# Columns of the modulation on TensorE: three more folded pairs, ten of VectorE's rows in the fold's bank, and a new order of VectorE's steps

## The reference, cut to what matters

```
cond = silu(c)
mod = cond @ w_ada[l] + b_ada[l]          # 2048 -> 6 * 2048
sh1, sc1, g1, sh2, sc2, g2 = split(mod)
u = x * (1 + sc1) + sh1
y = mixer(u)                              # layer 0: pooling and gated linear attention
x = layer_norm(ALPHA * x + (1 + g1) * y)
u = x * (1 + sc2) + sh2
y = conv_ffn(u)
x = layer_norm(ALPHA * x + (1 + g2) * y)
```

## Time and profile before

| | us |
|---|---|
| median of 3 runs | 2245.31 (2243.19 to 2245.43) |
| the profiled execution | 2243.39 |
| its span, first to last instruction | 2241.6 |
| TensorE busy in the span | 2208.9 |
| VectorE busy | 1683.4 |
| ScalarE busy | 1017.8 |

### The profile page before, as it was taken

One profiled execution on the slowest core, in us unless ns is written; L12 is line 12 of the kernel. 1 busy time (PEld: TensorE's weight loads), 2 busy tenths in 40 slices (PEclk: granted clock), 3 DMA queues, 4 the chain that ended last, 5 costly groups with the idle time before them and its releaser, 6 DMA issues.

```text
span 2241.6 us, 27926 instructions
## 1 busy us (share of the span) xinstructions
PE 2208.9 (99%) x11177; PEld 1836.6 (82%) x11177; DVE 1683.4 (75%) x1671; ACT 1017.8 (45%) x1050; POOL 15.6 (1%) x23
## 2 busy tenths in 40 slices
PE   7999999999999999999999999999999999999999
PEld 3778777788888888888788888878888888888886
DVE  2899999778878878788887767685788755565565
ACT  2445344454533444443455544445545334454432
POOL 1000000000000000000000000000000000000000
PEclk9999999999999999999999999999999999999999
DMA  9999899968889888789887877866688766556652
GB/s 377 385 406 350 308 329 353 318 212 276 298 300 355 301 276 288 261 281 331 309 292 277 293 260 248 309 217 190 210 275 300 258 203 197 189 187 190 236 186 102
DMA packets 392907, 612.70 MB, mean 273 GB/s; under 512 B 21229, under 2 KB 205221, under 8 KB 391750
## 3 DMA queue, kind: packets, MB, share of 16 engines
q1 hardware_dynamic: 387994, 608.34, 77.7%
q10 hardware_dynamic: 4336, 2.33, 0.3%
q0 software_dynamic: 448, 0.25, 0.0%
HBM read 608.71 MB, written 2.13 MB: 273 GB/s over the span
## 4 chain that ended last, share of the span: by engine, by line
PE 58%; DVE 1%; issue 0%; ACT 0%; DVEq 0%; ACTq 0%
PE banks L1654 32%; PE banks L1805 14%; PE banks L1813 7%; PE banks L1690 1%; PE banks L2130 1%; DVE w_lo L1050 0%; PE banks L2225 0%; PE banks L2192 0%; PE banks L2213 0%; PE banks L2202 0%; PE banks L1914 0%; PE banks L2265 0%; PE banks L2260 0%; PE banks L1758 0%; DVE ada_acc L1078 0%
## 5 line engine op out<-in xcount | busy, mean ns | idle before, releaser
L1050 DVE TENSOR_TENSOR w_lo<-w_raw,w_hi 128x2048 fp32r<-128x2048 f32 (+2 forms) x377 | 840.6, 2232 | 347.0 <-ACT w_hi L657 300.1
L657 ACT ACTIVATE w_hi<-w_raw 128x2048 fp32r<-128x2048 f32 (+2 forms) x377 | 703.9, 1869 | 759.3 <-PE banks L1654 439.4
L1805 PE MATMUL banks<-u_hl,w_hi 128*128 128x512 f32 x2368 | 573.1, 391 | 0.0
L1805 PEld LDWEIGHTS banks<-u_hl,w_hi 128*128 128x128 f32 x2368 | 432.9, 188 | 84.5 <-issue 1.2
L1654 PE MATMUL banks<-w_hi,u_hl 128*128 128x512 f32 x1792 | 439.3, 397 | 9.5 <-ACT u_hl L724 4.3
L1654 PEld LDWEIGHTS banks<-w_hi,u_hl 128*128 128x128 f32 x1792 | 333.9, 190 | 86.1 <-issue 11.7
L1813 PEld LDWEIGHTS banks<-u_hl,w_lo 128*128 128x128 f32 x2368 | 308.4, 191 | 15.5 <-DVE w_lo L1050 1.2
L1813 PE MATMUL banks<-u_hl,w_lo 128*128 128x256 f32 x2368 | 313.2, 283 | 0.3 <-DVE w_lo L1050 0.3
L1654 PE MATMUL banks<-w_hi,hid_hi 128*128 128x512 f32 x660 | 257.7, 390 | 0.0
L1654 PE MATMUL banks<-w_hi,hid_lo 128*128 128x512 f32 x660 | 256.9, 389 | 0.0
L1078 DVE SCALAR_TENSOR_TENSOR ada_acc<-ada_w,silu_c,ada_acc 128x1024 f32<-128x1024 f32 x187 | 239.2, 1279 | 22.1 <-DMA ada_w<-in_w_ada 16.2
(11 more groups left out here) (273 smaller groups left out, 1373.5 us busy)
## 6 DMA issues: line engine op xcount, KB each, us to landing
ada_w<-in_w_ada SPq DMA_DIRECT2D x352, 512.0 KB, 7.0
w_raw<-in_w_up SPq DMA_DIRECT2D x344, 512.0 KB, 4.8
w_raw<-in_w_down SPq DMA_DIRECT2D x152, 512.0 KB, 5.1
w_raw<-in_w_qkv SPq DMA_DIRECT2D x96, 512.0 KB, 4.9
w_raw<-in_w_in_ab SPq DMA_DIRECT2D x64, 512.0 KB, 9.2
ada_w_more<-in_w_ada SPq DMA_DIRECT2D x32, 512.0 KB, 10.7
w_raw<-in_w_out_ab SPq DMA_DIRECT2D x32, 512.0 KB, 6.6
w_raw<-in_w_o SPq DMA_DIRECT2D x32, 512.0 KB, 5.1
```

Source lines behind the costliest of these rows:

```text
L657: nc.scalar.activation(hi_at(u)[:, 0:width], raw[:, u % RAW_SLOTS, 0:width], ACT.Copy).then_inc(w_hi, 1)
L1050: nc.vector.tensor_tensor(lo_at(u)[:, 0:width], raw[:, u % RAW_SLOTS, 0:width], hi_at(u)[:, 0:width].bitcast(f32), ALU.subtract).then_inc( ...
L1805: ins = nc.tensor.matmul(bank[banks[s] + i][:, :], tile(w_h, k, s, i), uhl[:, kt].rearrange("p a s -> p (a s)"), start=first and k == 0, s ...
```

## The change

Pairs 3, 6 and 7 are folded as well. For pairs 3, 4, 5 and 7 the last 4, 2, 2 and 2 rows (PE_LAST) are no longer VectorE's: in `ada_fold` TensorE multiplies each straight from its load slot, as four matmuls of 32 stationary columns (a column of `silu_c`, repeated) and 256 moving ones, into the bank in which the matmuls with ones then add VectorE's accumulator. The load into such a row's slot waits for `a_on_pe`. The folds move: pair 3's is at the end of unit 15, pair 4's at the end of unit 22 (before: 23), pair 5's at 29 (before: 30), pairs 6 and 7 at 39 and 41, their sums at 40 and 42 (before: 39 and 41). The gate copies of pairs 4 and 5 come one unit earlier, at loads 30 and 37. On VectorE, pair 2's evacuation moves from slot 12 to the end of slot 11; the low part of unit 15 moves from slot 13 into slot 12, ahead of that slot's rows; the scores stand ahead of `lo_unit` from slot 30 on; and the rows of slot 36 come in slot 37, behind `mix_lo`.

```diff
--- before.py
+++ after.py
@@ -95,6 +95,7 @@
 POOL_MEAN = {26: (0, 1), 28: (2, 3)}
 POOL_MAP = {27: (0, 1), 29: (2, 3)}
 Y_B_T = {36: (4, 5), 37: (6, 7)}
+ROWS_LATE = 36
 
 
 
@@ -141,11 +142,14 @@
 LATE_PAIRS = (9, 8)
 LATE_SUM = 8
 GATE_PAIRS = (4, 5, 10, 11, 18, 19, 22, 23)
-FOLDED = (2, 4, 5, 8, 10, 11, 12, 13, 14, 15, 16, 17, 18, 19, 20, 21, 22, 23)
+FOLDED = (2, 3, 4, 5, 6, 7, 8, 10, 11, 12, 13, 14, 15, 16, 17, 18, 19, 20, 21, 22, 23)
 WARM_SUMS = {0: 18}
 
 PE_ROWS = {0: 12, 1: 12, 9: 10}
-PE_BASE = {0: 0, 1: 12, 9: 24}
+PE_LAST = {3: 4, 4: 2, 5: 2, 7: 2}
+PE_BASE = {0: 0, 1: 12}
+for _m in (3, 4, 5, 7, 9):
+    PE_BASE[_m] = 24 + sum(PE_LAST.get(m, 0) for m in range(_m))
 PE_FIRST = 12
 UP_PIECES = {0: {4: (4, 5), 8: (6, 7)}, 1: {2: (4, 5), 3: (6, 7)}}
 AFTER_UP = {0: 7, 1: 21}
@@ -171,6 +175,8 @@
     fill(2, 3, [3, 3, 3, 3, 2, 2])
     fill(3, 9, [3, 3, 3, 3, 2, 2])
     fill(4, 15, [2, 2, 3, 2, 2, 3, 2, 2, 3, 2, 2, 3, 3, 4, 3, 2, 2, 3, 3, 2, 3, 3, 3, 3, 2])
+    for s in at:
+        at[s] = [(m, r) for m, r in at[s] if r < KT - PE_LAST.get(m, 0)]
     first = PH[0, "up_a"]["unit"]
     put([(8, r) for r in range(7)], first - 8, [1, 1, 2, 1, 2])
     loads[first - 3] = [(9, r) for r in range(4)]
@@ -192,11 +198,11 @@
     for n, m in enumerate((18, 19, 20, 21)):
         fill(m, first + (4, 18, 32, 47)[n], [1, 2, 1] * 4)
 
-    ends = {m: max(s for s in at if (m, KT - 1) in at[s]) for m in range(1, len(ADA_PAIRS))}
+    ends = {m: max(s for s in at if (m, KT - 1 - PE_LAST.get(m, 0)) in at[s]) for m in range(1, len(ADA_PAIRS))}
     sum_at = {m: s + 2 for m, s in ends.items()}
     sum_at |= {m: ends[m] + 3 for m in (11, 23)} | {1: 2, 2: 12, 3: 16, 6: 39, 8: ends[8] + 1}
     sum_at |= {m: sum_at[m] + 1 for m in FOLDED if m > 6}
-    sum_at |= {m: sum_at[m] + 1 for m in (4, 5)}
+    sum_at |= {4: 23, 5: 30, 6: 40, 7: 42}
     folds = {sum_at[m] - 1: m for m in FOLDED}
     assert [folds[s] for s in sorted(folds)] == list(FOLDED)
     sums, number = {}, {0: 0}
@@ -476,6 +482,8 @@
                     of, k = ROW_OF[old]
                     if k < PE_ROWS.get(of, 0):
                         sp.wait_ge(a_on_pe, PE_BASE[of] + k + 1)
+                    elif k >= KT - PE_LAST.get(of, 0):
+                        sp.wait_ge(a_on_pe, PE_BASE[of] + k - (KT - PE_LAST[of]) + 1)
                     else:
                         sp.wait_ge(a_step, A0 + old + 1)
                 w = A["w_ada"][layer].rearrange("(k p) (s n c) -> p k s n c", p=P, s=6, n=4)
@@ -598,6 +606,7 @@
                     gate_bias(0, 2)
                 if v == 20:
                     sp.wait_ge(a_step, A0 + 4 * KT)
+                    sp.wait_ge(a_on_pe, PE_BASE[3] + PE_LAST[3])
                     sp.dma_start(sums_in[:, :], A["sums"]).then_inc(sem("pool_in"), 16)
                     sp.dma_start(band[:, :, :], A["band"]).then_inc(sem("pool_in"), 16)
                     for g in range(4):
@@ -1075,8 +1084,10 @@
                     nc.vector.tensor_scalar(acc[:, :], w, silu_c[:, 0:1], None, ALU.mult).then_inc(a_step, 1)
                 else:
                     dve.wait_ge(a_step, A0 + ROW_NO[m, r - 1] + 1)
-                    nc.vector.scalar_tensor_tensor(acc[:, :], w, silu_c[:, r:r + 1], acc[:, :],
-                                                   ALU.mult, ALU.add).then_inc(a_step, 1)
+                    ins = nc.vector.scalar_tensor_tensor(acc[:, :], w, silu_c[:, r:r + 1], acc[:, :],
+                                                         ALU.mult, ALU.add)
+                    on_pe = PE_LAST.get(m, 0)
+                    ins.then_inc(a_step, 1 + on_pe if r == KT - 1 - on_pe else 1)
 
             def ada_evac(m):
                 layer, part, n = ADA_PAIRS[m]
@@ -1519,6 +1530,7 @@
                     nc.vector.tensor_tensor(w_lrl, w_lr[:, :, :], w_lrh.bitcast(f32), ALU.subtract
                                             ).then_inc(sem("lr_lo"), 1)
                 if s == 16:
+                    dve.wait_ge(a_on_pe, PE_BASE[3] + PE_LAST[3])
                     nc.vector.memset(lrT[:, :], 1.0).then_inc(sem("lr_one"), 1)
                 if s in FULL_SLOT:
                     n = FULL_SLOT[s]
@@ -1535,10 +1547,20 @@
                 if s - 1 in Y_B_T:
                     for v in Y_B_T[s - 1]:
                         mix_lo(v)
+                if s - 1 == ROWS_LATE:
+                    rows_of(s - 1)
                 if s in HEAD_S1:
                     head_decay(HEAD_S1[s])
-                if s < FRONT_UNITS - 1:
+                if s == 30:
+                    dve.wait_ge(t_full, T_MIX + 4)
+                    nc.vector.memset(scT[:, :, :, :], 0.0).then_inc(sem("sc_zero"), 1)
+                    dve.wait_ge(sem("sc_zero"), 1)
+                if s in HEAD_S2:
+                    gla_scores(HEAD_S2[s])
+                if s < FRONT_UNITS - 1 and s != 13:
                     lo_unit(s + 2)
+                if s == 12:
+                    lo_unit(s + 3)
                 if s in OUT_LAST:
                     out_tail(OUT_LAST[s])
                 if s == GATE_SLOT + 1:
@@ -1547,18 +1569,18 @@
                         ins = nc.vector.scalar_tensor_tensor(loga[:, t, :], T[t][:, :], 0.0, kdec[:, t, :],
                                                              ALU.min, ALU.subtract)
                     ins.then_inc(sem("log_a"), 1)
-                if s == 30:
-                    dve.wait_ge(t_full, T_MIX + 4)
-                    nc.vector.memset(scT[:, :, :, :], 0.0).then_inc(sem("sc_zero"), 1)
-                    dve.wait_ge(sem("sc_zero"), 1)
-                if s in HEAD_S2:
-                    gla_scores(HEAD_S2[s])
                 if s in HEAD_S3:
                     gla_norm(HEAD_S3[s])
                 if s == 34:
                     dve.wait_ge(sem("gla_n"), GH)
                     nc.vector.tensor_scalar(gvar, gmv[:, :, 1], EPS, None, ALU.add).then_inc(sem("gla_var"), 1)
-                if s > 1:
+                if s == 11:
+                    evacs(s + 1)
+                if s == 12:
+                    rows_of(s)
+                elif s == ROWS_LATE:
+                    evacs(s)
+                elif s > 1:
                     beside(s)
                 if s == 34:
                     dve.wait_ge(sem("gla_var"), 1)
@@ -1753,11 +1775,20 @@
                     pe.wait_ge(a_fold_out, FOLDED.index(m))
                 if m == 2:
                     pe.wait_ge(sem("xT_out"), 8)
-                to = fold_bank(m)
-                for q in range(4):
-                    ins = nc.tensor.matmul(to[32 * q:32 * q + 32, 0:2 * P], ones,
-                                           acc[:, 2 * P * q:2 * P * (q + 1)], start=True, stop=True)
-                ins.then_inc(a_fold, 1)
+                to, on_pe = fold_bank(m), PE_LAST.get(m, 0)
+
+                def quarters(weights, of, first, last):
+                    for q in range(4):
+                        ins = nc.tensor.matmul(to[32 * q:32 * q + 32, 0:2 * P], weights,
+                                               of[:, 2 * P * q:2 * P * (q + 1)], start=first, stop=last)
+                    return ins
+
+                for r in range(KT - on_pe, KT):
+                    slot, loads = ada_slot(m, r)
+                    pe.wait_ge(a_loaded[slot], 16 * loads)
+                    quarters(silu_c[:, r:r + 1].broadcast_to((P, 32)), ada_row_at(slot), r == KT - on_pe, False
+                             ).then_inc(a_on_pe, 1)
+                quarters(ones, acc, not on_pe, True).then_inc(a_fold, 1)
 
             def beside(s):
                 if s in ADA_FOLDS:
```

## The result

The changed kernel takes 2252.02 us (median of 7 runs, 2249.42 to 2253.06), the kernel before 2244.91 us (7 runs, 2242.82 to 2245.43): ratio 1.0033, 95% interval 1.0024 to 1.0042. It is 7.1 us slower, where the forecast was +3.0 us and a range that ended at 2251.5 us. So the prediction was wrong: "within 0.2%" was the likeliest side, and the time lies 0.5 us above the upper end.

What follows compares the result with a forecast made beforehand. With TensorE busy 99%, VectorE's list was taken to set the front's end: 1.4 + 5.1 - 2.56 - 0.96 = +3.0 us, so 2245.31 + 3.0 = 2248.3 us; 8-in-10 range 2239.5 to 2251.5 us.

Steps and rivals of the forecast that it cites:

- within 0.2%: Outcome for the whole kernel: time changes by no more than 4.5 us either way; chance 0.5.
- the step up to the fold of pair 5: Front up to pair 5's fold: rows +2.5, pair 3 -1.0, old stalls -3.34, new stall +3.2, sum +1.4 us.
- F: Time at which TensorE starts pair 5's fold; today's counterpart is 248.73 us, forecast to move by +1.4 us.
- the slot of (5,14): Load (6,2) waits for TensorE to free this slot at pair 5's fold; VectorE loses 5.1 us.
- the 4.6 us of the earlier trace: Landing time taken for load (6,2), as into a nearly idle queue; up to 6.5 us for the range.
- the clock falls in the new stall: Rival at pair 3's fold: TensorE's clock drops, 2.1 us lost, +5.1 us in all, 2250.4 us; chance 0.2.
- TensorE waiting at the first scores: Sign of being right: after pair 5's fold TensorE waits at the scores; no size given.
- what ends the front: VectorE's low part of unit 47, with TensorE waiting for it, was to end the front +3.0 us later.
- The load wait of 0.96 us at 305 us: VectorE's idle time for a load before unit 47's low part, counted as regained: -0.96 us.
- TensorE not idle between 360 and 371 us: Sign of being wrong, near the front's end; would put the time near 2241 us.
- Every us there passes into the total: From the front's end, where the layer norm starts, each us of delay was to count fully in the total.
- Folds and sums move: Pairs 3, 6 and 7 folded: 0.70 us each for a plain sum's 1.70, -3.0 us on TensorE.

Runs made afterwards that it cites:

- one row: Changed kernel with only row (5,15) of pair 5 on TensorE, (5,14) with VectorE: 2247.67 us, ratio 1.001.
- the earlier fold: Changed kernel with pair 5's fold one unit earlier, at the end of unit 28: 2248.44 us, ratio 1.0017.
- the fastest version: Changed kernel with pair 5's rows back on VectorE, pair 6's evacuation early, pair 3 folded at the end of unit 16: 2239.63 us, ratio 0.9976.

## Why the prediction was wrong

**Right: the step up to the fold of pair 5, as a chain.** The stalls of units 15 and 18 are gone, and pair 3's rows wait for `ada_w_more` for 3.44 us (forecast 3.2). Rows cost 0.43 to 0.45 us (0.42), sums 0.70. F is 250.97 us, +3.5 us from the common point where the forecast had +1.4; 1.6 us of the difference is the fallen clock.

**Right: the slot of (5,14).** SyncE's queue stands at (6,2) as forecast, and VectorE idles for the load. The two timelines:

```profile
232.35 19.69 SPq L491 DMA_DIRECT2D ada_w<-in_w_ada  x4
252.08 0.98 SPq L496 DMA_DIRECT2D w_raw<-in_w_out_ab  x2
```

```profile
255.55 1.28 DVE L1087 SCALAR_TENSOR_TENSOR ada_acc<-ada_w,silu_c,ada_acc 128x1024 f32<-128x1024 f32 x1 [7.29 <-DMA ada_w<-in_w_ada]
```

The group of four loads took 2.72 us and takes 19.69 us now, the last of them issued at 251.7 us. VectorE is done with (6,2) at 256.83 us, F + 5.9 us (forecast F + 6.5). The load came 3.9 us after its issue, not 4.6, as the tile view of `ada_w` from 232 to 252.1 us has it:

```profile
DMA to landing us min/median/max: 3.9/7.7/12.1
```

The Trainium skill's fit for GpSimd's path ("DMA: Bandwidth & Descriptors", Anatomy of one DMA), an estimate of 3.2 us for these bytes, is still short of it on SyncE's queue: the measured landing lies between the fit and the 4.6 us of the earlier trace rows, and it is the fastest of its group, whose median is 7.7 us. The transfers had run dry while SyncE stood, as the window shows (DMA share 0.00, 0 GB/s):

```profile
248.00:252.00 4.00, 4.00 (x35) 3.00 (x37) 0.26 (x1) 2.36 (x6) 0.00 (x0) 1.00 0.00 0
```

The 4.6 us of the earlier trace rows were not those of a nearly idle queue, as the prediction had it: the DMA share was 1.05 from 264 to 266 us there. The error was 0.7 us, and on the safe side.

**Wrong: the clock.** This is the step that failed. The forecast was added up at full clock, and *the clock falls in the new stall* stood beside it as a rival at 0.2, for pair 3's stall alone, at 2.1 us. It fell there, and cost 1.6 us: the size was fair, the chance was not. This moves F, and with it VectorE, which waits for (6,2). Follow VectorE's list, which the prediction let decide: +3.5 us at F (forecast +1.4), +4.5 us more for (6,2) (forecast +5.1), and 2.58 us back up to the low part of unit 47 (forecast 3.52) make +5.4 us from the common point, where the forecast had +3.0. The row that carried the low chance was the one stall of 2.78 us at 316.76 us that left the clock at 1.00; among the runs here such a row is the rarer case (below). The Trainium skill ("TensorE: Matmul & The Clock Gate", The HAM clock gate) warns of idle gaps in a stream of matmuls; of 26 stalls of 2.09 to 3.52 us in these runs, 18 agree.

**Not priced: the second fall.** The clock fell again behind the first scores, for 3.1 us on TensorE. "TensorE waiting at the first scores" was written down as something to see and had no term. But not all of the 3.1 us pass into the total. VectorE was through with the low part of unit 47 at 373.02 us (370.73 + 2.29), 0.7 us before TensorE took it, and on the way it had waited only 0.6 us for TensorE (0.23) or for ScalarE, itself held by TensorE (0.37). So without the second fall the front would have been shorter by about 1.3 us at most; then TensorE would have stood for VectorE. The run with only the evacuation of pair 6 early agrees: 1.70 us of waiting taken off TensorE made this part of the front 1.1 to 1.4 us shorter and left a wait of 0.47 us for VectorE. This is worked out, and no run took the second fall away by itself.

**Wrong: what ends the front.** The prediction let VectorE's low part of unit 47 set the end, with TensorE waiting for it. VectorE got back just the two rows of slot 39 (2.58 us). The load wait of 0.96 us at 305 us is gone, but 0.89 us of other waits took its place (0.29 us for a load at 260.53, 0.23 for TensorE at 282.83, 0.37 for ScalarE at 358.71), so the 0.96 us of the sum was no gain. TensorE takes the low part without a bracket, 4.83 us after its counterpart at 368.91. With slow stretches of 4.7 us in all it was the later of two engines that are within 1 us of each other, +5.9 us against +5.4. TensorE not idle between 360 and 371 us was the prediction's own sign of being wrong, and it was to put the time near 2241 us. The sign came, and the time went the other way: a slow TensorE shows it as well as an early VectorE.

**Left out: the stretch behind the front.** "Every us there passes into the total" puts nothing behind the layer norm. With the front's +5.9 us alone the time would be 2250.8 us, inside the range. But against the one trace of the kernel before, all eleven others are longer behind the layer norm, by 1.1 to 6.6 us, the profiled execution of the changed kernel by 3.9 us.

**Missed: the wait before pair 7's fold,** 1.70 us for an evacuation behind the output's tail. "Folds and sums move" was costed by their matmuls, and what stands ahead of the evacuation on VectorE was not looked up. By itself it costs nothing that a median shows, and 1.1 to 1.4 us in the traces, until VectorE, nearly as late, stands in the way. It mattered more where TensorE was ahead (3.2 to 3.5 us with one row or with the earlier fold).

**The sum.** On TensorE's side it is +1.4 at F as forecast, +1.6 for the clock, -0.3 for four rows and two sums, -5.0 for the old stalls behind F, +4.5 for the new ones and +3.1 for the clock again: +5.3 us of the 5.9 measured. The two spans differ by 8.3 us: -1.3 us ahead of the common point, +5.9 us in the front, +3.9 us from there to the second layer, 3.0 us of it in the two waits near 700 us, and -0.2 us to the end. How the 7.1 us between the medians divide is not known, since one execution of each kernel was traced.

**Open: the waits for `w_lo` near 700 us.** There SyncE stands for pair 10's gate copy from 678.1 to 684.8 us, and `w_raw` comes late. The kernel before has this copy too, but SyncE is held for 5.2 us there and not for 6.7. TensorE's waits for `w_lo` follow that length: in the five traces with 6.7 to 7.5 us between the copy's two transfers they are 1.7 to 3.2 us in all, in the seven with 5.2 to 6.1 us they are 0 to 1.2 us. They are absent in the kernel before and in the fastest, and present in the other ten traces. The changed kernel has 6.7 us in one execution and 7.2 in the other. No run took this stretch by itself, so whether the longer copy belongs to the change or to the single execution is not known. Nor was it tried to move pair 3's loads earlier in SyncE's list.

## What to carry to other kernels

Moving work to another engine also moves the release of its buffer. Where loads go out of one in-order queue, a slot freed late by the slower consumer holds everything behind it: put the step where its loads have landed, and let an engine that is through early free the slots that are wanted first. And where TensorE stalls for about 2 us or more, price not only the stall but the matmuls behind it at the lower clock. Here the six old stalls (8.3 us) left the clock alone, and the three new ones (7.9 us) cost 4.7 us more. Then follow both engines to the point where they meet: what one of them loses counts only as far as it is the later one.

## What the runs showed of the hardware

**Stalls and the granted clock.** Take every stall of TensorE of 1 us or more between 100 and 710 us, in the traces of before, after and the ten experiments. Of those of 2.09 to 3.52 us, 26 in all, 18 have a window of 10 us at their end or right behind it with a granted clock of 0.58 to 0.89, and 8 left it at 1.00. None of the 15 between 1.0 and 1.9 us changed it. Within the upper group the length does not decide: 2.13 us cost the clock in one trace (0.83) and 3.23 us in another did not. Nor is 2 us a border: near 64 us all twelve traces have a stall of 1.93 to 2.85 us, eight of them under 2 us, and in every one the 16 matmuls behind it took 5.3 to 6.6 us in place of 3.8.

Eight of the traces have the same work and the same order up to unit 17, with pair 3 folded at unit 15. In six of them the clock fell at this fold, behind stalls of 2.7 to 3.4 us, and they took 35.98 to 36.78 us from the common point to the end of unit 17. In two it held, behind 2.24 us and behind 2.11 and 0.88 us, and they took 33.57 and 33.62 us. Two of the eight can be compared directly, since their stalls before unit 17 sum to the same 2.94 us: pair 5's fold earlier with the evacuation early, where the clock fell (36.30 us), and one row of pair 5, where it held (33.57 us). The fall cost 2.7 us.

So whether a given stall costs 2 to 3 us more may be partly chance from one execution to the next, which would also widen the runs of one kernel: those of the fastest version, which has no stall of 2 us in this range, spread over 4.4 us, those with pair 5's fold one unit earlier over 9.5. This last step is argued, not shown. Of the executions that were not profiled only the mean granted clock is known: 0.996 to 0.998 for the fastest version, 0.994 to 0.997 for the other, whose slowest execution has the lowest value. But executions of it at 0.995 to 0.997 still lie 7.2 us apart, so the clock is at most a part of the spread.

**Four strips at once.** 8 matmul records of 256 columns into four strips of 32 output partitions took 0.43 to 0.45 us, in line with the 0.42 us taken from the fold's row.
